# Half of the second layer's condition moved from the first MLP to the norm behind the state-space block

## What is computed

```python
def first_block(x, c, ctx, c_ctx, ...):
    xl, xc = x, ctx
    for li in range(DEPTH):                      # DEPTH = 2
        last = li == DEPTH - 1
        mod_l = jnp.split((jax.nn.silu(c) @ ada_w[li] + ada_b[li])[:, None, :], 6, axis=-1)
        mod_c = jnp.split(jax.nn.silu(c_ctx) @ ada_w[li] + ada_b[li], 6, axis=-1)
        hl = rmsnorm(xl, norm1_g[li]) * (1.0 + mod_l[1]) + mod_l[0]
        hc = rmsnorm(xc, norm1_g[li]) * (1.0 + mod_c[1]) + mod_c[0]
        # layer 0: hybrid_mixer, layer 1: ssd_mixer  -> ol, oc
...
        xl = xl + mod_l[2] * ol
        hl = rmsnorm(xl, norm2_g[li]) * (1.0 + mod_l[4]) + mod_l[3]
        xl = xl + mod_l[5] * sq_relu_mlp(hl, mlp_w1[li], mlp_w2[li])
...
    return rmsnorm(xl, norm_f_g)
```

## Time and profile before

| | |
|---|---|
| median of 3 runs | 2241.14 us (2240.78 to 2241.39) |
| the profiled execution, its own time | 2248.06 us |
| its span | 2246.3 us |
| PE busy | 2196.9 us, 98% |
| DVE, ACT, POOL busy | 53%, 23%, 7% |
| mean granted clock of PE | 0.982 of full |

### The profile page before, as it was taken

One profiled execution on the slowest core, in us unless ns is written; L12 is line 12 of the kernel. 1 busy time (PEld: TensorE's weight loads), 2 busy tenths in 40 slices (PEclk: granted clock), 3 DMA queues, 4 the chain that ended last, 5 costly groups with the idle time before them and its releaser, 6 DMA issues. The chain is left out here.

```text
span 2246.3 us, 40031 instructions
## 1 busy us (share of the span) xinstructions
PE 2196.9 (98%) x17594; PEld 1748.7 (78%) x17594; DVE 1181.3 (53%) x2226; ACT 515.2 (23%) x1087; POOL 159.0 (7%) x180
## 2 busy tenths in 40 slices
PE   8999899999999999999999999999999999999999
PEld 5444699994688888885666667899988877789999
DVE  2464654444645655755555644487534253228884
ACT  3233732221100000014434433100011143302200
POOL 0003032220000000001211211000000000000000
PEclk9999999999999999999999999999999799999999
DMA  7222022221322245332212211545453422234443
GB/s 313 71 75 75 20 79 79 79 78 38 113 78 91 96 190 204 132 142 83 75 61 73 93 57 60 204 170 178 169 188 131 143 83 95 75 132 151 169 169 132
DMA packets 38246, 260.68 MB, mean 116 GB/s; under 512 B 4647, under 2 KB 6327, under 8 KB 7480
## 3 DMA queue, kind: packets, MB, share of 16 engines
q1 hardware_dynamic: 34416, 248.83, 30.6%
q10 hardware_dynamic: 2760, 6.11, 0.7%
q0 software_dynamic: 896, 3.18, 0.4%
HBM read 256.49 MB, written 1.08 MB: 115 GB/s over the span
## 5 line engine op out<-in xcount | busy, mean ns | idle before, releaser
L182 PE MATMUL pairs<-h_sb,ring_sb 128*128 128x512 f32 (+1 forms) x976 | 329.3, 499 | 1.6 <-ACT h_sb L568 0.9
L182 PEld LDWEIGHTS pairs<-h_sb,ring_sb 128*128 128x128 f32 x976 | 187.9, 194 | 141.0 <-issue 123.7
L1771 PE MATMUL pairs<-h_sb,ring_sb 128*128 128x512 f32 (+1 forms) x784 | 265.1, 494 | 0.0
L1771 PEld LDWEIGHTS pairs<-h_sb,ring_sb 128*128 128x128 f32 x784 | 147.8, 191 | 106.6 <-issue 95.5
L306 PE MATMUL pairs<-mid 128*128 128x128 f32 (+1 forms) x1232 | 182.2, 303 | 0.6 <-DVE mid L348 0.6
L306 PEld LDWEIGHTS pairs<-mid 128*128 128x128 f32 x1232 | 166.7, 193 | 9.4 <-issue 1.2
L326 DVE TENSOR_TENSOR mid<-ring_sb 128x512 f32<-128x512 f32 (+1 forms) x98 | 66.9, 682 | 119.3 <-DMA ring_sb<-weights 65.0
L182 PE MATMUL pairs<-big,ring_sb 128*128 128x256 f32 (+1 forms) x576 | 123.7, 381 | 3.4 <-DVE one L2843 2.8
L182 PEld LDWEIGHTS pairs<-big,ring_sb 128*128 128x128 f32 x576 | 110.8, 217 | 16.5 <-DVE one L2843 3.2
L306 PE MATMUL pairs<-h_sb,ring_sb 128*128 128x128 f32 (+1 forms) x736 | 107.4, 298 | 3.0 <-ACT h_sb L568 2.3
L2060 DVE SCALAR_TENSOR_TENSOR big<-pairs,vec_table,big 128x508 f32<-128x508 f32 (+3 forms) x128 | 76.9, 674 | 62.1 <-ACT big L1961 62.0
(11 more groups left out here) (504 smaller groups left out, 3541.2 us busy)
## 6 DMA issues: line engine op xcount, KB each, us to landing
ring_sb<-weights SPq DMA_DIRECT2D x237, 1024.0 KB, 4.8
x_sb<-tokens ACTq DMA_DIRECT2D x1, 2048.0 KB, 11.8
mid<-bias_table POOLq DMA_DIRECT2D x1, 1536.0 KB, 6.9
const_table<-consts ACTq DMA_DIRECT2D x1, 1200.0 KB, 10.1
mid<-bias_table POOLq DMA_DIRECT2D x1, 1024.0 KB, 11.7
out<-x_sb ACTq DMA_DIRECT2D x4, 256.0 KB, 2.5
lora_w<-lora ACTq DMA_DIRECT2D x1, 512.0 KB, 13.4
vec_table<-vectors SPq DMA_DIRECT2D x1, 285.0 KB, 16.3
```

The lines of the kernel that those rows point to most:

```text
L182: last = pe.matmul(out, w[:, k, c, :], rhs(j * kt + k), start=(j == 0 and k == 0), stop=(j * kt + k == k_end - 1))
L1771: ins = pe.matmul(m.pairs[:, at % 2, c, 0:T], w[:, k, c, :], m.h[:, k, TOK - T:TOK], start=(k == 0), stop=(k == 7))
```

## The change

Half 8 of the second layer's condition leaves tiles 7 and 8 of `mlp0_down`. Halves 8 and 9 now stand behind the last tile of `mlp0_down`, where 9 and 10 stood, and halves 10 and 11 both behind `ssd_out`. On PE, the rows of halves 10 and 11 now stand ahead of the norm sums and the two turns behind the spread of the root; the filler matmul is gone. Half 11 has its rows in a bank of its own (`bank[:, 2, :]`) and is marked as apart, so that its rows don't wait for half 10's copies. ScalarE copies half 10's rows ahead of the root and half 11's behind it. VectorE adds the bias to halves 4 to 9 ahead of `ssd_out`'s residual and to 10 and 11 in the second MLP.

```diff
-ADA1_AFTER = {("hy_out", 3): (0,), **{("mlp0_down", n): (n + 1,) for n in range(8)}, ("mlp0_down", 15): (9, 10),
-              ("ssd_out", 7): (11,)}
+ADA1_AFTER = {("hy_out", 3): (0,), **{("mlp0_down", n): (n + 1,) for n in range(7)}, ("mlp0_down", 15): (8, 9),
+              ("ssd_out", 7): (10, 11)}
...
 def ada_rows_pe(s, m, li, half, between=None):
...
-    if at:
+    if at and not (li and m.ada_apart(li, half)):
         pe.wait_ge(sem["rows_out"], 2 * at)
...
 def ada_turn_pe(s, m, li, half):
...
-    if at:
+    if at and not (li and m.ada_apart(li, half)):
         pe.wait_ge(sem["mods_copied"], at)
...
     def conditions(n, last):
-        if not last and 1 <= n <= 8:
+        if not last and 1 <= n <= 7:
             ada_turn_pe(s, m, 1, n)
-        if last and n < 8:
+        if last and n < 7:
             ada_rows_pe(s, m, 1, n + 1)
...
     pe.wait_ge(sem["first_out"], FIRST_OUT_AT["mlp0_down", 3])
+    ada_rows_pe(s, m, 1, 8)
+    ada_turn_pe(s, m, 1, 8)
     ada_rows_pe(s, m, 1, 9)
-    ada_turn_pe(s, m, 1, 9)
-    ada_rows_pe(s, m, 1, 10)
     norm_sums_pe(s, m, m.h[:, 0, :])
     norm_rows_pe(s, m, TOK)
-    ada_turn_pe(s, m, 1, 10)
+    ada_turn_pe(s, m, 1, 9)
...
     for n in range(2, 4):
         product_group_pe(s, m, "ssd_out", n, lambda k: m.y_fm[:, k, :], SEQ)
+    ada_rows_pe(s, m, 1, 10)
     ada_rows_pe(s, m, 1, 11)
-    busy_pe(s, m, m.bank[:, 3, :], 1)
     norm_sums_pe(s, m, m.h[:, 0, CTX:TOK])
     norm_rows_pe(s, m, SEQ)
+    ada_turn_pe(s, m, 1, 10)
     ada_turn_pe(s, m, 1, 11)
...
-    ada_dve(s, m, 1, (4, 11), [(1, "norm2_1", 4)])
+    ada_dve(s, m, 1, (4, 10), [(1, "norm2_1", 4)])
...
-        return li == 0 and half < 4
+        return half < 4 if li == 0 else half == 11
...
-            bank = self.bank[:, 0, :] if 1 <= half <= 8 else self.pair4[:, 0, :] if 9 <= half <= 10 else self.bank[:, 1, :]
+            bank = self.bank[:, 0, :] if 1 <= half <= 7 else self.pair4[:, 0, :] if 8 <= half <= 9 else \
+                self.bank[:, 2, :] if half == 11 else self.bank[:, 1, :]
...
             residual_squares_act(s, m, "ssd_out", CTX, TOK, lambda k: [(m.h[:, k, CTX:TOK], 1.0)])
             act.wait_ge(sem["mods_ready"], s.next("mods_ready"))
+            ada_rows_act(s, m, 1, 10)
+            norm_root_act(s, m, SEQ)
             ada_rows_act(s, m, 1, 11)
-            norm_root_act(s, m, SEQ)
+            ada_mods_act(s, m, 1, 10)
             ada_mods_act(s, m, 1, 11)
             norm_act(s, m, ada_parts(m, 1, 1, LATENT))
```

More of the change, by code:

```diff
@@ L782, in down0_act @@
             first_out_act(s, m, "mlp0_down", n // 4)
-        if 1 <= n <= 8:
+        if 1 <= n <= 7:
             ada_mods_act(s, m, 1, n)
-        if n < 8:
+        if n < 7:
             ada_rows_act(s, m, 1, n + 1)
@@ L789, in down0_act @@
             if g == 3:
-                ada_rows_act(s, m, 1, 9)
+                ada_rows_act(s, m, 1, 8)
             act.wait_ge(sem["x_ready"], s.next("x_ready"))
@@ L793, in down0_act @@
             if g == 3:
-                ada_mods_act(s, m, 1, 9)
+                ada_mods_act(s, m, 1, 8)
             act.wait_ge(sem["dve_emptied"], EMPTIED_BEFORE["mlp0_down"] + g + 1)
@@ L829, in conditions @@
         if li == 1 and g == 0:
-            ada_dve(s, m, 1, (11, 12), [])
+            ada_dve(s, m, 1, (10, 12), [])
     if li == 0:
@@ L3318, in _ @@
             down0_act(s, m)
-            ada_rows_act(s, m, 1, 10)
+            ada_rows_act(s, m, 1, 9)
             act.wait_ge(sem["mods_ready"], s.next("mods_ready"))
             norm_root_act(s, m, TOK)
-            ada_mods_act(s, m, 1, 10)
+            ada_mods_act(s, m, 1, 9)
             norm_act(s, m, ada_parts(m, 1, 0, BOTH))
```

## The result

| | median of the timed runs | against the kernel before |
|---|---|---|
| before, as first timed | 2241.14 us | |
| before, with one run more beside the changed kernel | 2240.96 us (4 runs) | |
| changed | 2257.56 us (2253.99 to 2259.35, 4 runs) | 1.0075, 95% interval 1.0059 to 1.0091 |

The change makes the kernel 16.6 us slower. The direction was forecast, the size was not: 10.2 us were forecast, and 2257.56 lies above the range (2247.0 to 2254.5). The two profiled executions, 2248.06 us before and 2256.69 us after, stand only 8.6 us apart, about half of what the medians say. Why they do is the first thing to find out.

The account below looks back on a forecast made before the run. PE, busy 98% of the span, was taken to bound the kernel. The terms -2.95 + 9.99 + 3.45 - 0.3 = +10.2 us, carried over to the 2241.14 us median, gave 2251.3 us; 8-in-10 range 2247.0 to 2254.5.

Parts of the forecast that it names:

- What bounds the kernel, and which wait is last: PE is busy 98% of the span; VectorE's sums of tile 130, ahead of ssd_out's last group, hold the norm.
- the rule of the ring: Behind ssd_out, tile 130's load is issued when tile 126, after the edit half 10's first tile, has been used.
- Part 1: First MLP: half 8's rows and turn leave its seventh and eighth tile, -2.95 us (bounds -2.95 and -2.0).
- Part 2: Behind ssd_out: tile 130 lands at 1439.83 instead of 1429.84, delaying the norm sums by +9.99 us.
- (d): Behind ssd_out: longer low clock or tile 130 up to 1.6 us later, +11.8 to +14, 2253 to 2255 us; 9%.
- Part 3: Norm sums to the second MLP's first matmul: second turn and low clock, +3.45 us (bounds +0.95 and +4.2).
- Part 4: Start of the second MLP: PE loses half the low-clock stretch, 2.9 us before, 2.4 to 2.9 after: -0.3 us.
- (a): Behind ssd_out: tile 130 in time, PE's extra rows lie in the wait; -2.0 us, 2239.1 or 2238.2 us; 3%.
- (b): Behind ssd_out: VectorE not held, PE waits for the last condition tile; +1.1 us, 2242.2 us; 4%.
- (c): Behind ssd_out: stall at full clock, or back at once when work resumes; +7.7 or +5.1, 2246.2 to 2248.8 us; 12%.
- (e): First MLP: no PE time is removed, VectorE gives it all back; +13.2 us, 2254.3 us; 2%.

Follow-up runs that it names:

- the wait alone: The kernel before, with VectorE's sums of tile 130 also waiting until tile 132 or tile 131 has landed: 2253.74 us (1.0064) or 2248.51 us (1.0031).
- the fillers: The changed kernel with filler matmuls on constants in PE's waits behind ssd_out: 2248.57 us, ratio to before 1.0048.

## Why the prediction missed

**What bounds the kernel, and which wait is last: right.** The place, the engine, the tile and the rule of the ring came out as said. The version with half 10 inside `ssd_out`, and the wait alone put into the kernel before, show it from both sides: the loss goes with the late tile, and comes with a late tile alone.

**Part 1, -2.95 us: right.** The first MLP's stretch went from 419.6 to 416.6 or 416.7 us in five of the eight profiles that have the changed kernel's order there. In the other three it took 417.0 to 417.5; in two of these the clock fell at the last condition rows. VectorE gave nothing back.

**Part 2, +9.99 us: 10.6 to 11.0, nearly right.** Tile 130 landed 7.6 and 7.9 us after its issue in the two profiles, not 7.1. One more load stands in the queue behind it, which I had in rival (d) and left out of the sum. The load in the same place took 7.1 and 6.9 us in the kernel before, and 6.2 in both kernels with the wait alone, all without the further load; whether that load is the reason isn't shown by itself. The estimate worked out from the Trainium skill's fit (DMA: Bandwidth & Descriptors, section Anatomy of one DMA) has it landed 6.8 us behind the issue of the load ahead of it; the trace shows 8.6 (1426.46 to 1435.09). The row of before, 8.1 us by the same count, lay nearer.

**Part 3, +3.45 us: right, +3.3.** Each turn took 1.7 us at the low clock, where 1.9 was put. The reason given there for the fall of the clock in the trace of before, a stretch with little for PE to do, is not in its rows: PE was busy for 1.76 and 1.45 us of the 2 us from 1433 and from 1435, and the clock fell at 1437.0. What sets it off stays open.

**Part 4 and the base of the sum: wrong, and this is the step that failed.** The sum was made against one execution, 2248.06 us, and then carried over to the median. Against that execution it is nearly right: +10.2 forecast, +8.6 measured between the two profiles, and +10.9 in the stretches that the sum speaks of (-3.0, +10.6, +3.3, 0.0). But that execution had the low clock for 6.8 us at the very place of the edit, and more of it elsewhere. The second profile, of an execution near the usual 2239.7 us, has 3.4 us of it there.

The price of that low clock was too high as well. The sum took half of the low time under work, 2.9 us today. The second MLP takes 201.4 us where the clock held, 201.8 in the second profile of before and 203.1 in the first, so it cost 0.4 and 1.7 us. One reason shows in the rows above: the first 16 matmuls take 3.03 us even at the full clock, and not the 1.95 of the earlier trace rows, because their weight loads wait for ScalarE to scale h. So the clock term, put at -0.3, is 0 against the first profile and +1.0 to +1.3 against the second (201.8 to 202.9 and 203.1). I saw that the profile stood 0.3% over the median, took it for a constant of the profiler, and didn't ask which stretches made the difference. The same mistake narrowed the range: the two bounds were worked out from terms, and neither had the spread of executions, which the 7 us between a profile and its own median showed before any run.

How much of the miss that is can be read from the two profiles nearest to the medians, the second ones, 2240.46 and 2256.07 us, 15.6 us apart. In them the four terms come to -2.0, +11.0, +3.3 and +1.0, together +13.4 before rounding, where +10.2 was forecast. The other 2.2 us lie in stretches that the sum put at nothing: +2.4 in the norm behind the first MLP, +0.8 and +0.6 in the norm behind the second MLP and the products of the second block, -0.5 in the state-space block and -1.1 ahead of the first MLP.

**What stays open.** Why those other stretches differ. The mean granted clock is about 0.981 in the changed kernel's timed runs and 0.986 in before's, some 23 us more at the low clock, of which 17 lie in the stall (20.5 against 3.4). One place says more when all 13 profiles are laid side by side. At the norm behind the second MLP the clock was low for 6.8 us in seven of them and not at all in six. The seven include all five in which the norm sums of the place of the edit came 9.8 us or more behind `ssd_out` (the changed kernel twice, the fillers, both waits alone), and only two of the other eight (the first profile of before, half 8 moved alone). That norm and the products behind it take 152.8 to 156.2 us in the seven, and 149.9 to 151.6 in the six. So the stall probably makes a low stretch 200 us later more frequent, at 1 us or more; how it would do that, no run shows. The norm behind the first MLP, 4.9 to 7.8 us, has no such order in the profiles.

**The rivals.** (a), the gap is filled, was rightly held small; (b) exists as a second wait behind the first; of (c) nothing was seen, the clock was low from 1432.0 to 1452.4; (d) was right in that the tile came later than in the sum, by 0.5 to 0.8 us, and its time (2253 to 2255) was still short; (e) was wrong.

## What to carry to other kernels

In a ring, the place of a tile is a date for every tile behind it: moving work between two places that PE finds equal can put the next stage's first tile behind it, so look for who waits for that tile, and above all for an in-order engine on which the wait stands ahead of something that others need. When the profiled execution is not at the median, find first which stretches make it so, and price each term of a sum against what those stretches usually take. A stretch at the low clock need not cost half of its length: at the start of the second MLP, where PE follows ScalarE's pieces anyway, 3.4 us of it cost 0.4 us and 6.8 us cost 1.7. Two otherwise equal places for the same work, two tiles apart in the order of the ring, differed here by 16 us.

## What the runs showed of the hardware

The same program took 2233 to 2249 us, and its time went with the mean granted clock, 0.981 to 0.989, at 1.7 us per 0.001. Around norms in which PE stands for less than a microsecond at a time, the low clock came or not: in two executions of the kernel before it lasted 6.8 and 3.4 us at the norm behind `ssd_out`, and 6.8 us and not at all at the norm behind the second MLP. In the stall of the changed kernel it lasted 20.5 us in both profiles. And a load of 1 MB behind another that was issued 1.03 us earlier landed after 7.1 and 6.9 us in two executions of the kernel before, after 6.2 in the two kernels with the wait alone, and after 7.6 and 7.9 in the changed kernel, so even a landing read from one trace is good to a microsecond only.
